# First tile of routed rows made from the token rows in SBUF by one-hot products on TensorE

## The reference, cut to what matters

```
t = rms_norm(hres) .reshape(-1, 1024)               # 520 token rows
pg = softmax(t @ rg_w + rg_b); g = top-1 of 4 groups
e  = top-2 of the 4 experts in that group; wts = softmax(their logits) * pg[g]
h  = silu(t @ w1[e]) * (t @ w3[e])                  # 1024 -> 256, 16 experts in all
y  = hres + sum over the two experts of wts * (h @ w2[e])
```

## Time and profile before

| | us |
|---|---|
| median of 3 runs (lowest, highest) | 797.73 (796.99, 797.9) |
| profiled execution | 797.19 |
| its span, first to last instruction | 795.3 |
| PE busy | 762.9 (96%) |
| DVE busy | 378.9 (48%) |
| ACT busy | 224.6 (28%) |
| POOL busy | 295.1 (37%) |

### The profile page before, as it was taken

One profiled execution on the slowest core, in us unless ns is written; L12 is line 12 of the kernel. 1 busy time (PEld: TensorE's weight loads), 2 busy tenths in 40 slices (PEclk: granted clock), 3 DMA queues, 4 the chain that ended last, 5 costly groups with the idle time before them and its releaser, 6 DMA issues.

```text
span 795.3 us, 14291 instructions
## 1 busy us (share of the span) xinstructions
PE 762.9 (96%) x5269; PEld 544.4 (68%) x5269; DVE 378.9 (48%) x714; ACT 224.6 (28%) x435; POOL 295.1 (37%) x221
## 2 busy tenths in 40 slices
PE   9999899999999999999999999999999789999992
PEld 7887678766677888777777787888887634333330
DVE  4636676777488679544543112734533712030210
ACT  4130343441423355133414222422201511020100
POOL 0000232264653974344434555534241122333314
PEclk9999999999999999999999999999999999999996
DMA  9242463345665542155534453351670899999943
GB/s 365 113 160 82 139 210 109 105 158 163 172 182 188 164 150 67 55 162 183 168 127 125 145 182 136 101 190 68 248 281 20 319 322 405 378 384 370 383 134 50
DMA packets 72538, 148.32 MB, mean 187 GB/s; under 512 B 13335, under 2 KB 47144, under 8 KB 70420
## 3 DMA queue, kind: packets, MB, share of 16 engines
q1 hardware_dynamic: 65716, 135.43, 48.8%
q0 software_dynamic: 5920, 10.82, 5.4%
q10 hardware_dynamic: 832, 1.16, 0.6%
HBM read 137.71 MB, written 18.90 MB: 197 GB/s over the span
## 4 chain that ended last, share of the span: by engine, by line
PE 87%; DVE 6%; ACT 2%; DMA 2%; issue 1%; POOLq 0%; POOL 0%; ACTq 0%; SPq 0%; DVEq 0%
PE ps L874 22%; PE ps L608 14%; PE ps L1210 11%; PE ps L843 7%; PE ps L1118 6%; PE ps L1280 5%; PE ps L651 3%; PE ps L623 3%; PE ps L900 2%; PE ps L678 1%; PE ps L1199 1%; PE ps L597 1%; PE ps L707 1%; PE ps L694 1%; DMA tmp<-in_xT 1%
## 5 line engine op out<-in xcount | busy, mean ns | idle before, releaser
L608 PE MATMUL ps<-xn,ring 128*128 128x268 f32 (+1 forms) x576 | 136.6, 392 | 0.2 <-ACT qk L1373 0.2
L608 PEld LDWEIGHTS ps<-xn,ring 128*128 128x128 f32 x576 | 106.9, 190 | 24.7 <-issue 3.7
L2569 POOL TENSOR_TENSOR kv<-kv,sgd 128x1024 f32<-128x1024 f32 (+1 forms) x32 | 79.8, 2511 | 100.9 <-DVE tmp L1845 51.5
L1529 ACT ACTIVATE sgt<-sgt,vec 128x260 f32<-128x260 f32 x60 | 30.1, 510 | 123.5 <-DVE sgt L2125 72.3
L2684 POOL DMA_INDIRECT out_y<-cst,gtab x24 | 37.3, 1555 | 71.0 <-DVE cst L2494 42.5
L843 PE MATMUL ps<-br,ring 128*128 128x260 f32 x256 | 60.9, 386 | 0.8 <-DVE sgt L2129 0.8
L874 PE MATMUL ps<-xn,ring 128*128 128x260 f32 x240 | 58.0, 385 | 0.0
L874 PE MATMUL ps<-xn,qb 128*128 128x260 f32 x240 | 57.6, 383 | 0.1
L843 PEld LDWEIGHTS ps<-br,ring 128*128 128x128 f32 x256 | 47.9, 190 | 11.4 <-issue 3.2
L874 PEld LDWEIGHTS ps<-xn,qb 128*128 128x128 f32 x240 | 45.4, 190 | 7.4 <-issue 0.4
L874 PEld LDWEIGHTS ps<-xn,ring 128*128 128x128 f32 x240 | 45.0, 190 | 7.4 <-issue 0.4
(11 more groups left out here) (524 smaller groups left out, 1493.7 us busy)
## 6 DMA issues: line engine op xcount, KB each, us to landing
ring<-in_w_mg SPq DMA_DIRECT2D x32, 640.0 KB, 4.5
kv<-in_kc SPq DMA_DIRECT2D x128, 128.0 KB, 2.1
kv<-in_vc SPq DMA_DIRECT2D x128, 128.0 KB, 2.1
ring<-in_w_in SPq DMA_DIRECT2D x24, 512.0 KB, 4.9
kv<-in_w SPq DMA_DIRECT2D x8, 1024.0 KB
br<-in_w SPq DMA_DIRECT2D x7, 1024.0 KB
sgd<-in_w SPq DMA_DIRECT2D x6, 1024.0 KB, 12.1
qk<-in_w SPq DMA_DIRECT2D x6, 1024.0 KB, 12.0
```

The source lines that it names most:

```text
L608: mm = pe.matmul(ps[:, 2 * (t % 2) + h, 0:hw], wsl(c, k), xnv[:, k, col0 + h * hw:col0 + (h + 1) * hw], start=(k == 0), stop=(k == KT - 1))
L1529: act.activation(g, g, ACT.Sigmoid, bias=vv(V_BM + 8 * "ABCD".index(n) + m + i)).then_inc(g_a, 1)
L2569: pool.tensor_tensor(kb, kb, qbc[:, b:b + 1, :].to_broadcast([P, HALF // 2 + (half and u), 256]), ALU.mult)\
```

## The change

- Five `tk` buffers: blocks 0 and 1 in cg and cx, blocks 2 to 4 in cst; sgt and dqk are no longer among them.
- The one-hot tables start 3072 columns into ring, and `pick` (2 x 5 x 128 columns) is new in ring.
- DVE makes `pick` after `oh_row`: for each choice a compare of `pos_f` with 0 to 127, that is, one where the token is row r of tile 0, and the sum of both choices.
- PE's `picked(h, blocks)` multiplies the token rows of a block, `tk[b]`, with `pick`: the sum over five blocks is tile 0 already transposed, in bank 3 (lower half) and bank 6 (upper half). It takes the place of gather(0), rows_T(0) and rows_T(1).
- The last two residual blocks are transposed ahead of the table products. The weight marks and the weight table are put into `hidden_first`.
- DVE's `rows_copy(0)` comes before the tables' remaining work. Gathers begin with tile 1; the waits that count them are set accordingly. ACT waits for `g_ok` only ahead of its first scaled copy.

```diff
--- before.py
+++ after.py
@@ -257,7 +257,7 @@
         rw32, ms32, fold32, n2c = view(g0, 0, KT, 32), view(g0, 256, 32), view(g0, 288, 32), view(g0, 320, KT)
         lgT = view(ea, 500, N)
         hres = [view(xn, b * DM, DM)[0:RB] for b in range(4)] + [bg[0:RB, 0:DM]]
-        tk = [t[0:RB, 0:DM] for t in (cg, sgt, dqk)] + [view(cst, C_DT + i * DM, DM)[0:RB] for i in range(2)]
+        tk = [cg[0:RB, 0:DM], cx[0:RB, 0:DM]] + [view(cst, at, DM)[0:RB] for at in (C_COS, C_DT, C_DT + DM)]
         lg = view(ea, 0, NB, 20)
         rt = view(ea, 100, 20, NB, 4)
         f12 = view(dr, 0, 2, NB, 4, 4)
@@ -271,8 +271,10 @@
         io_row, io_tile = view(dr, 720, P), view(dr, 720 + P, TILES + OVER + 1)
         tri4 = view(dr, 1040, 16)
         n_t = TILES + OVER
-        oh_row, oh_tile = view(ring, 0, 10, P), view(ring, 10 * P, 2, NB, n_t)
-        steps, marks = view(ring, 10 * (P + n_t), 10, n_t + 1), view(ring, 10 * (P + 2 * n_t + 1), 4, NB, 32)
+        oh_at = ROUNDS * DM
+        oh_row, oh_tile = view(ring, oh_at, 10, P), view(ring, oh_at + 10 * P, 2, NB, n_t)
+        steps, marks = view(ring, oh_at + 10 * (P + n_t), 10, n_t + 1), view(ring, oh_at + 10 * (P + 2 * n_t + 1), 4, NB, 32)
+        pick = view(ring, DM, 2, NB, P)
         from_row, to_row, to_row2 = [gtab[:, i * (n_t + OVER):(i + 1) * (n_t + OVER)] for i in range(3)]
         s1, s2 = view(qb, 0, 512), view(qb, 512, 512)
         os1, os2 = [[view(t, 512 * i, 4, P) for t in (bg, dv)] for i in range(2)]
@@ -332,6 +334,7 @@
         lgm, rank_ok, tab_t, tab_sum, tab_tt, wts_t, wts_tt = [(route_t, i + 1) for i in range(7)]
         rw_ok, lg_t, lg_a, lg_d = sem("rw_ok"), sem("lg_t"), sem("lg_a"), sem("lg_d")
         r1, r2, sel_ok, idx_ok = sem("r1"), sem("r2"), sem("sel_ok"), sem("idx_ok")
+        pick_ok = [(xms, 2), (xms, 3)]
         xs_ok, idx2_ok, oh_ok, oh2_ok, tab_ok, g_ok = [sem(k) for k in ("xs_ok", "idx2_ok", "oh_ok", "oh2_ok", "tab_ok", "g_ok")]
         m_w = [sem(f"m_w{i}") for i in range(STREAM)]
         m_xe, m_yst = [sem(f"m_xe{i}") for i in range(ROUNDS)], [sem(f"m_yst{i}") for i in range(ROUNDS)]
@@ -543,7 +546,7 @@
                 sp.dma_start(scr_x[b * RB:(b + 1) * RB, :], tk[b]).then_inc(xs_ok, 16)
             for b in range(3):
                 residual(b)
-            sp.wait_ge(m_xe[0], 16)
+            sp.wait_ge(m_xe[1], 16)
             for b in range(3, NB):
                 residual(b)
             sp.wait_ge(tt_t, 2 * NB)
@@ -1165,7 +1168,7 @@
                 pe.matmul(rank[:, b + 1:, :], every[:, 0:RB], selm[:, b:b + 1, :].to_broadcast([RB, NB - 1 - b, NE]),
                           start=False, stop=(b == NB - 2))
             pe.matmul(ps[:, 5, 0:NB * NE], every, selm, start=True, stop=True).then_inc(rank_ok[0], 1)
-            for b in range(3):
+            for b in range(NB):
                 rows_of(hTr, b, NB + b)
             for b in range(NB):
                 pe.wait_ge(oh_ok, 2 if b < 3 else 3)
@@ -1173,20 +1176,39 @@
                     mm = pe.matmul(ps[32 * j:32 * j + 32, 5, 0:P], marks[0:RB, j, b, :], oh_row[0:RB, NB * j + b, :],
                                    start=(b == 0), stop=(b == NB - 1), tile_position=(0, 32 * j))
             mm.then_inc(tab_t[0], 1)
+
+            def picked(h, blocks):
+
+                for b in blocks:
+                    pe.wait_ge(*pick_ok[b >= 3])
+                    for k in range(4):
+                        mm = pe.matmul(ps[:, 6 if h else 3, k * P:(k + 1) * P], tk[b][:, (4 * h + k) * P:(4 * h + k + 1) * P],
+                                       pick[0:RB, 0, b, :], start=(b == 0 and k == 0), stop=(b == NB - 1), skip_group_check=True)
+                if NB - 1 in blocks:
+                    mm.then_inc(m_t, 1)
+
+            pe.wait_ge(tt_a, NB + 3)
+            picked(0, range(3))
             pe.wait_ge(sel_ok, 2)
             pe.matmul(ps[:, 4, 0:n_t], slots[0:64], fold32[0:64, 0:n_t], start=True, stop=True).then_inc(tab_sum[0], 1)
             pe.transpose(ps[:, 5, P:P + 64], slots[0:64], ident[0:64, 0:64]).then_inc(tab_tt[0], 1)
-            rows_of(hTr, 3, NB + 3)
-            rows_of(hTr, 4, NB + 4)
-            pe.wait_ge(oh_ok, 4)
-            pe.wait_ge(tt_a, NB + 3)
-            for b in range(NB):
-                for j in range(2):
-                    mm = pe.matmul(ps[32 * j:32 * j + 32, 2, 0:P], marks[0:RB, 2 + j, b, :], oh_row[0:RB, NB * j + b, :],
-                                   start=(b == 0), stop=(b == NB - 1), tile_position=(0, 32 * j))
-            mm.then_inc(wts_t[0], 1)
-            pe.wait_ge(sel_ok, 3)
-            pe.matmul(ps[:, 2, P:P + n_t], slots[0:64], fold32[0:64, 0:n_t], start=True, stop=True).then_inc(wts_tt[0], 1)
+            picked(0, range(3, NB))
+            pe.wait_ge(tt_a, NB + 4)
+            picked(1, range(NB))
+
+            def weight_marks():
+
+                pe.wait_ge(oh_ok, 4)
+                for b in range(NB):
+                    for j in range(2):
+                        mm = pe.matmul(ps[32 * j:32 * j + 32, 2, 0:P], marks[0:RB, 2 + j, b, :], oh_row[0:RB, NB * j + b, :],
+                                       start=(b == 0), stop=(b == NB - 1), tile_position=(0, 32 * j))
+                mm.then_inc(wts_t[0], 1)
+
+            def weight_table():
+
+                pe.wait_ge(sel_ok, 3)
+                pe.matmul(ps[:, 2, P:P + n_t], slots[0:64], fold32[0:64, 0:n_t], start=True, stop=True).then_inc(wts_tt[0], 1)
 
             def rows_T(u):
 
@@ -1194,7 +1216,7 @@
                 if u >= 3:
                     pe.wait_ge(m_ta if u % 2 else m_td, (u - 3) // 2 + 1)
                 if h == 0:
-                    pe.wait_ge(m_xe[i % ROUNDS], 16 * (i // ROUNDS + 1))
+                    pe.wait_ge(m_xe[i % ROUNDS], 16 * (i // ROUNDS + (i % ROUNDS > 0)))
                 for k in range(4):
                     mm = pe.transpose(ps[:, 3 + u % 3, k * P:(k + 1) * P], xe[i % ROUNDS][:, (4 * h + k) * P:(4 * h + k + 1) * P], ident)
                 mm.then_inc(m_t, 1)
@@ -1222,9 +1244,12 @@
                         pe.wait_ge(m_td, 1)
                     mm = hidden_one(0, k)
                     if k == 3:
+                        weight_marks()
+                    if k == 5:
                         rows_T(2)
                         rows_T(3)
                 mm.then_inc(m_h1, 1)
+                weight_table()
                 rows_T(4)
                 rows_T(5)
                 for k in range(KT):
@@ -1282,8 +1307,6 @@
                     mm.then_inc(m_y, 1)
 
             pe.wait_ge(tt_a, 2 * NB)
-            rows_T(0)
-            rows_T(1)
             for q in range(QUADS):
                 u, i = 2 * ROUNDS * (q + 1), ROUNDS * q
                 more = q < QUADS - 1
@@ -1313,7 +1336,7 @@
                 pe.wait_ge(m_yd, TILES)
                 with pe.Fori(0, n_over) as i:
                     pe.wait_ge(o_ld, i * 32 + 32)
-                    pe.wait_ge(m_xe[0], i * 16 + 16 * (QUADS + 1))
+                    pe.wait_ge(m_xe[0], i * 16 + 16 * QUADS)
                     for k in range(KT):
                         mm = pe.transpose(ps[:, 3 + k // 4, (k % 4) * P:(k % 4 + 1) * P], xe[0][:, k * P:(k + 1) * P], ident)
                     mm.then_inc(o_pe, 1)
@@ -1701,11 +1724,11 @@
                 act.wait_ge(m_h1, i + 1)
                 act.activation(si[i % ROUNDS], ps[:, i % ROUNDS, 0:256], ACT.Silu).then_inc(m_si, 1)
 
-            act.wait_ge(g_ok, 1)
-
             def out_copy(i):
 
                 last = i >= TILES - ROUNDS
+                if i == 0:
+                    act.wait_ge(g_ok, 1)
                 act.wait_ge(m_y, 2 * i + 1)
                 if i >= ROUNDS:
                     act.wait_ge(m_yst[i % ROUNDS], 32 * (i // ROUNDS))
@@ -2430,10 +2453,21 @@
                    io_row[R].unsqueeze(1).unsqueeze(1).to_broadcast([RB, 2, b1 - b0, P]),
                    each.unsqueeze(3).to_broadcast([RB, 2, b1 - b0, P]), ALU.is_equal).then_inc(oh_ok, 1)
 
+            def rows_copy(i):
+
+                dve.wait_ge(m_t, 2 * i + 2)
+                dve.tensor_copy(xeT[i % (2 * ROUNDS)][:, 4:8, :].rearrange("p k n -> p (k n)"), ps[:, 3 + (2 * i + 1) % 3 if i else 6, :])\
+                  .then_inc(m_td, 1)
+
             def two_kinds(kind, bk):
                 dve.wait_ge(*kind)
                 dve.tensor_copy(slots[0:64, :], ps[0:64, bk, 0:P]).then_inc(sel_ok, 1)
 
+            for n, (b0, b1) in enumerate(((0, 3), (3, NB))):
+                link(tt(pick[0:RB, :, b0:b1, :], io_row[0:RB].unsqueeze(1).unsqueeze(1).to_broadcast([RB, 2, b1 - b0, P]),
+                        pos_f[R, :].rearrange("p (n b) -> p n b", n=2)[:, :, b0:b1].unsqueeze(3).to_broadcast([RB, 2, b1 - b0, P]),
+                        ALU.is_equal))
+                tt(pick[0:RB, 0, b0:b1, :], pick[0:RB, 0, b0:b1, :], pick[0:RB, 1, b0:b1, :], ALU.add).then_inc(pick_ok[n][0], 1)
             two_kinds(tab_t, 5)
             kinds = [slots[:, 64 + 32 * j:64 + 32 * j + n_t] for j in range(2)]
```

(11 more changed lines are left out.)

## The result

The changed kernel took 802.75 us (median of 6 executions, 801.38 to 803.27); the kernel before, beside it, 797.57 (796.99 to 798.75). The ratio is 1.0048, with a 95% interval of 1.0029 to 1.0066: slower. Two later comparisons of the same two kernels gave 1.0020 (0.9998 to 1.0042, so not told from no change) and 1.0029 (1.0013 to 1.0046). Over all executions, on several chips, the median is 801.5 for the change (30) and 798.6 for before (110): 2.9 us, not 5.2.

The account below looks back on a forecast made before the run. PE, with 87% of the chain, was taken as the bound. At the start of tiles 1 and 2 the terms 1.37 - 1.47 + 1.3 + 0.06 gave +1.3 us, so 799.0 from a median of 797.73; range 797.0 to 801.0.

Parts of the forecast that it names:

- Part 1: Last 16 residual transposes moved into PE's idle time ahead of the table products: cost 0, 2.0 us without that cover.
- Part 2: DVE makes pick ahead of the table copy: first half ready at 632.4, second at 633.4; DVE's delay itself costs nothing.
- Part 3: Picks on PE: 80 instructions at 0.1116, 8.93 us, replacing the gather wait; first expert matmul 1.37 us later.
- Rivals B, C and D: Picks on PE, in order: at transposes' cost, 10.3 us (0.08); at L1165's pace, 6.8 (0.11); one instruction each, 5.1 (0.06).
- Part 4: First 32 expert instructions: PE without pause keeps the clock at 1.00, so 3.57 us instead of 5.04, -1.47.
- rival A: Low clock comes anyway, under the picks or at the first expert matmuls: +2.8 us, 800.5; chance 0.17.
- Part 5: Weight marks (1.1) and weight table (0.22) in the expert stream, no longer hidden: +1.3 us, plus 0.06 behind DVE's copy.
- Part 6: Gathers' row numbers 3.0 us later, SP's stores and weight loads behind them, all through before PE needs them: cost 0.

Follow-up runs that it names:

- before_hole: The kernel before with nine extra 128 x 128 matmuls in PE's idle stretches between the weight marks and the first transposes of gathered rows; 801.28 us.
- marks_ahead: The changed kernel with the weight marks and weight table ahead of the expert matmuls again, behind the picks; 804.03 us.
- before_same: The kernel before, unedited, run again as a control; 798.23 us.
- pick_half: The changed kernel with the picks of the upper half left out but one (2 instructions for 40); 801.48 us.
- before_again: The kernel before, unedited, a third look; 798.03 us.
- after_again: The changed kernel, unedited, run again beside the unedited kernel before; 801.44 us.
- before_filled: The kernel before with extra 128 x 128 matmuls in two of PE's idle stretches, 82 to 84 and 636.6 to 639 us; 800.50 us.

## Why the prediction was wrong

The sign was forecast, the size was not: +1.3 us, called not measurable, against 2.9 over all executions and 5.2 in the first comparison, which put 802.75 above the stated range. By its own steps:

- *Part 1 (transposes ahead of the table):* right. They were done before L1176, which still waited 0.75 us for DVE.
- *Part 2 (pick on DVE):* right to 0.1: first half ready 2.16 us after the table products' start, forecast 2.03.
- *Part 3 (picks):* 80 instructions, 0.112 each in a group, as taken from L651. Starts and the switch to the table sum add 0.4: 9.37 us of picks, forecast 8.93. From the first pick to the first expert matmul 9.78 us, forecast 9.36. Rivals B, C and D are refuted (10.3, 6.8 and 5.1 for the picks).
- *Part 4 (clock, -1.47):* **this is the step that failed.** In the first pair of traces it came out as forecast, 3.57 us for the first 32 expert instructions against 5.04. But the step took the fall at 640 of one execution for a fixed cost of the kernel before, to be saved by keeping PE busy, and the changed kernel's clock for safe. The three traces of the kernel before have the fall at 640, 635 and 633, and the later two hide most or all of it under the gather wait. Without a costly fall its S is 19.2 (20.62 less 1.47, and 19.18 where the wait covers the fall; 19.34 in before_hole). Over the three traces it is 19.9 on average. So the fall was priced at 1.5 where the three traces make it 0.7 on average. The kernels with picks had a fall in S in 3 of 7 traces, and there it costs 1.6 in full; rival A, taken as an alternative with a chance of 0.17, is a part of the usual course. In the three traces of the unedited change S is 22.48, 22.48 and 24.11, 23.0 on average.
- *Part 5 (marks and table into the stream):* 0.97 and the two instructions behind it (0.1) against 1.1; the table 0.33 against 0.22; no stall behind it (1.03 between L1221's and L1232's starts). Right to 0.1, and marks_ahead shows that the other place is dearer.
- *Part 6 (gathers, SP):* right; no PE wait for sgt or dqk.
- *The comparison itself:* I took 1.6 us as what can be told from no change, and the base for steady. The time of the kernel before goes from 794.75 to 803.91 over 110 executions, and two falls more or fewer in an execution (1.6 us each) are more than the whole effect. Of the 5.2 us between the first two traces, 2.86 come from one fall at 84, twice as long. Falls aren't the only thing that comes and goes: in before_same and pick_half PE waited 1.3 and 1.4 us for a weight load (br) in L1280 and L1306, and in no other trace. The first comparison had before at 797.6, a microsecond under its long median.

Without clock falls in S the price of the change is 22.48 - 19.2 = 3.3 us. Of this 1.9 lie ahead of the first expert matmul (11.94 us after the table products' start, against 10.03): the picks cost 9.4, where before PE had been idle for only 3.5 us between its table products and the experts, and the rest of what PE did there has moved or is gone. The other 1.4 are weight marks and weight table, formerly hidden. The forecast without its clock term had 2.7 for the same.

That the averages of S differ by 3.1 and the medians of all executions by 2.9 is in part luck, for S holds three traces of each kernel, and the rest of the program doesn't cancel. The mean granted clock of each execution shows it. It is 0.987 on average over 104 executions of before and 0.991 over the 30 of the change; a thousandth less is 1.6 us more at 1.2 GHz, so an execution of the change spends some 6 us less there (an estimate from these means). At the same mean clock the gap is wider: at 0.991 the spans are 793.4 to 794.8 (14 executions of before) and 799.1 to 800.0 (5 of the change), at 0.990 they are 794.9 to 796.6 (9) and 798.7 to 801.6 (8). So the kernel with picks is longer at the full clock, as part 4 supposed (in S, falls in 3 of 7 traces with picks and in 5 of 6 without), but no experiment shows that the fuller stretch is the reason, and it doesn't make up for the picks. Why the gap at one clock, 4.4 to 5.4 on average, is more than 3.3 stays open; falls that before hides under its wait, as in before_again, lower its mean clock without costing time and can be a part of it.

The Trainium skill (TensorE: Matmul & The Clock Gate, "Part 4: PE-mode transpose") says that transposes don't count as PE being busy for the clock in the way matmuls do. I set it aside because one trace stayed at 1.00 behind a stretch of them. before_again and after_again fall at 633, behind 24 and 40 transposes, an idle stretch and narrow table products: these agree with it, and one trace was too little to reject it. All 13 traces have such a stretch; in 7 the clock fell between 0.6 us ahead of the table products' start and 2.7 behind it, in 6 it did not, so the page's sentence alone doesn't forecast the fall either.

## What to carry to other kernels

A pause of PE behind a DMA is not only idle time: it also swallows clock falls and small table work. Before filling it, add up what is hidden there, and compare the new work with PE's idle time in the pause, not with the DMA's length (9.4 us of picks for a gather of 5.3, beside which PE was idle for 3.5). A clock fall seen in one trace is a sample, not a property of its line; take several traces of the unchanged kernel before crediting a change with its removal. Where chance moves whole times by more than the effect, compare a stretch between two fixed instructions, and set the mean granted clock of every execution beside its time.

## What the runs showed of the hardware

- The clock fell in up to four places of the same program while PE had work, in a different set in each execution. In the 13 traces: behind an idle stretch at 84 (7 traces; in the two with that stretch filled never), behind narrow matmuls (64 x 1 and 16-column ones) at 255 (5), behind 32-row and one-column ones at 407 to 410 (3), and in S (8). Each of these lasted 3.4 or 6.8 us. One of 3.4 us costs 1.6, one of 6.8 costs 3.1, if PE has work.
- A fall under the wait for the gather cost nothing (S = 19.18, before_again), and with that wait filled the same 6.8 us fall cost 1.7 (before_filled against before_hole) in place of 0.7 (before_same against before_again).
- In every trace the clock falls once more when PE's work is over (last matmul done at 781.2, fall at 783.3 in before) and stays at 0.50 to the end. This takes part of the mean clock and costs PE nothing.
- Over 104 later executions of before with their mean clock recorded, the span follows it: 793.4 to 794.8 at 0.991, 799.9 to 802.0 at 0.983.
- What decides in which execution a fall comes is open. No experiment here controlled it. With the stretch at 84 filled no fall came there in 2 of 2 traces; with the gather wait filled one came in S in 1 of 2; and neither lowered the time.
